# A decoder step's attention, rewritten: prompt heads in pairs on the array's halves, sample queries stationary, compression as filler

## What is computed

```python
z = x @ w_in
# mixer A, 8 heads x 64: stick-breaking attention
z = einsum('bthd,bshd->bhts', q, k) * SCALE
log_keep = where(mask, log_sigmoid(-z), 0)
cum = cumsum(log_keep); after = cum[..., -1:] - cum
o_a = where(mask, exp(log_sigmoid(z) + after), 0) @ v
# mixer B, 8 query heads in 2 groups: three softmax branches (compressed, selected, window)
blk = t[:, idx] + cmp_pe               # 15 blocks of 32 rows, stride 16, per sequence and group
ck, cv = gelu(blk @ cmp_w1) @ cmp_w2   # compressed keys and values
o_b = g0 * softmax(q ck) cv + g1 * softmax(q sk) sv + g2 * softmax(q wk) wv
# then, unchanged by the edit
m = concat(rms(o_a), rms(o_b)) @ w_out; h = LN(alpha*x + m)
y = LN(alpha*h + PEER(h))              # 16384 experts, top 16 of 8 heads
```

## Time and profile before

| | |
|---|---|
| median of 3 runs | 1209.02 us (1208.8 to 1218.2) |
| profiled execution | 1215.3 us, span 1213.2 us |
| PE busy | 1170.7 us (96%) |
| PE weight loads | 1029.2 us (85%) |
| DVE, ACT, POOL busy | 870.0, 580.8, 253.5 us |
| chain that ended last | PE 79%, DVE 8%, DMA 5%, issue 5% |

### The profile page before, as it was taken

The page is one execution under the profiler, slowest core; times in us unless marked ns, Lnnn a source line. Parts: engine busy times, 40 slices in busy tenths (PEclk is TensorE's granted clock), DMA queues, the critical chain, the costliest instruction groups (busy, mean ns, idle before and its releaser), DMA issues.

```text
span 1213.2 us, 23944 instructions
## 1 busy us (share of the span) xinstructions
PE 1170.7 (96%) x7404; PEld 1029.2 (85%) x7404; DVE 870.0 (72%) x1835; ACT 580.8 (48%) x1091; POOL 253.5 (21%) x264
## 2 busy tenths in 40 slices
PE   7999999999989999999999999998999999999996
PEld 7984787767879999999999999997878778788875
DVE  4320124324578898888775699997999989887777
ACT  5432753324444544444446455554555555555543
POOL 0425000003000010004540000001545555442330
PEclk9999875559989999999999999999999999999998
DMA  7758311001433578779998554445899989887772
GB/s 249 286 165 292 112 66 70 1 1 52 139 104 123 175 235 293 234 226 335 407 407 269 179 151 136 145 145 177 276 322 305 296 294 307 299 268 244 240 238 82
DMA packets 96361, 253.11 MB, mean 209 GB/s; under 512 B 11168, under 2 KB 43984, under 8 KB 95648
## 3 DMA queue, kind: packets, MB, share of 16 engines
q1 hardware_dynamic: 81840, 196.86, 49.2%
q0 software_dynamic: 14480, 55.75, 13.1%
HBM read 232.51 MB, written 22.12 MB: 210 GB/s over the span
## 4 chain that ended last, share of the span: by engine, by line
PE 79%; DVE 8%; DMA 5%; issue 5%; ACT 2%; POOL 1%; DVEq 0%; SPq 0%; ACTq 0%; POOLq 0%
PE ps L535 13%; PE ps L537 12%; PE ps L536 12%; PE ps L944 6%; PE ps L946 6%; PE ps L945 6%; PE ps L925 5%; DMA activations<-u_out 4%; DVE w_lo L1311 4%; PE ps L631 3%; PE ps L778 2%; DVE sacc L1745 1%; PE ps L658 1%; PE ps L764 1%; PE ps L871 1%
## 5 line engine op out<-in xcount | busy, mean ns | idle before, releaser
L1311 DVE TENSOR_TENSOR w_lo<-ring,w_hi 128x512 fp32r<-128x512 f32 (+1 forms) x458 | 430.2, 949 | 115.0 <-ACT w_hi L998 99.0
L998 ACT CAST w_hi<-ring 128x512 fp32r<-128x512 f32 (+1 forms) x460 | 344.2, 752 | 95.0 <-PE ps L946 49.7
L535 PE MATMUL ps<-h_hi,w_hi 128*128 128x256 f32 (+1 forms) x1152 | 339.9, 295 | 6.5 <-DVE h_lo L1572 4.9
L537 PE MATMUL ps<-h_hi,w_lo 128*128 128x256 f32 (+1 forms) x1152 | 326.7, 284 | 0.0
L536 PE MATMUL ps<-h_lo,w_hi 128*128 128x256 f32 (+1 forms) x1152 | 324.3, 282 | 0.0
L535 PEld LDWEIGHTS ps<-h_hi,w_hi 128*128 128x128 f32 x1152 | 218.2, 189 | 11.7 <-DVE h_lo L1572 5.3
L536 PEld LDWEIGHTS ps<-h_lo,w_hi 128*128 128x128 f32 x1152 | 218.2, 189 | 0.0
L537 PEld LDWEIGHTS ps<-h_hi,w_lo 128*128 128x128 f32 x1152 | 217.4, 189 | 0.0
L944 PE MATMUL ps<-w_hi,y_hi 128*128 128x512 f32 x512 | 201.1, 393 | 10.0 <-DVE y_lo L1733 9.2
L945 PE MATMUL ps<-w_hi,y_lo 128*128 128x512 f32 x512 | 200.0, 391 | 0.0
L946 PE MATMUL ps<-w_lo,y_hi 128*128 128x512 f32 x512 | 199.8, 390 | 0.0
(11 more groups left out here) (347 smaller groups left out, 1447.4 us busy)
## 6 DMA issues: line engine op xcount, KB each, us to landing
ring<-in_uT_dram SPq DMA_DIRECT2D x128, 512.0 KB
ring<-in_v_dram SPq DMA_DIRECT2D x128, 512.0 KB
activations<-u_out SPq DMA_DIRECT2D x128, 128.0 KB
a_in<-activations SPq DMA_DIRECT2D x128, 128.0 KB, 4.2
ring<-in_w_in_dram SPq DMA_DIRECT2D x22, 512.0 KB
kvs<-in_cache_sb_dram POOLq DMA_DIRECT2D x16, 512.0 KB, 7.0
ring<-in_w_q_dram SPq DMA_DIRECT2D x16, 512.0 KB
ring<-in_w_out_dram SPq DMA_DIRECT2D x8, 512.0 KB
```

The source lines that it names most:

```text
L535: mm(out, hi, hi_, start=start, stop=False)
L537: return mm(out, lo, hi_, start=False, stop=stop)
L998: nc.scalar.copy(w_hi[slot][:, x], ring[:, ring_slot, x]).then_inc(part_hi, 2 if half is None else 1)
L1311: V.tensor_tensor(w_lo[slot][:, x], ring[:, ring_slot, x], w_hi[slot][:, x].bitcast(F32), ALU.subtract).then_inc(part_lo[ring_slot], 2 if ...
```

## The change

Attention's list is rewritten on all engines; the projection, the output projection and the experts keep theirs.

- Prompt heads go in pairs p (two heads of 64 on the rows or columns 0 to 63 and 64 to 127 of the array): the two matmuls of a pair stand next to each other and write two banks (scores) or the two column halves of one bank (values). The `block` mask is added by DVE before the softplus, so the two mask products of `sb_sums` and the two `keep` multiplications go.
- ACT loads one table set that holds Exp and Ln, ahead of the loops, and does Abs, Exp, Ln on a pair (768 columns); the scaling of queries goes into ACT's copy out of the projection.
- The compression matmuls read 15 neighbouring elements per sequence. For that POOL copies the gathered pages into that layout (two `tensor_copy` of 2048 elements per partition), and only then issues the rest. The 32 matmuls are cut into 8 parts and stand between the steps of the stick-breaking pairs.
- Sample scores and values: queries or weights (32 columns per sequence) are stationary, cached keys and values move (256 or 512 columns); four sequences use the four column strips of the array. Scores then lie with rows on the partitions, so 6 transposes turn them (`zrow`), and for the values a mask (`picked`) and 8 small products (`tokrow`) pick each head's part.
- The loop over the softmax heads goes in 4 pairs; the transposes of the compressed weights stand in `np_turn` (8 transposes instead of 6).
- The closing sample value products are reordered so that four sequences stand next to each other.
- POOL's DMAs: `nsk` right after the copies, keys (16) and values (8 and 8) as separate half pages, the window cache earlier, the 2 MB output copy last. Issues of pages grow from 48 to 64.

```diff
             for n in range(PAGES):
-                b, p = n // 2, n % 2
-                pool.dma_start(cmpT[:, 2 + 2 * b:4 + 2 * b, :, 64 * p:64 * p + 64].rearrange("p g k n -> p (g k) n"),
-                               src(cache_cmp, n).rearrange("a p g k n -> (a p) (g k) n")).then_inc(cmp_in, 16)
-            pool.wait_ge(w_mm, 2 * N_IN)
-            for n in range(PAGES):
-                pool.dma_start(kvs[:, n, :], src(cache_sb, n).rearrange("a p c -> (a p) c")).then_inc(kv_in[n // 4], 16)
+                pool.dma_start(pages_in[:, n // 2, n % 2, :, :],
+                               src(cache_cmp, n).rearrange("a p w c -> (a p) w c")).then_inc(cmp_in, 16)
+            pool.wait_ge(cmp_in, 16 * (PAGES + 1))
+            for p in range(2):
+                nc.gpsimd.tensor_copy(
+                    cmpT[:, 2:2 + 2 * NB, :, :, 8 * p:8 * p + 8].rearrange("q (b g) k m a -> q b (g k) m a", g=2),
+                    pages_in[:, :, p, :, :]).then_inc(cmp_laid, 1)
+            pool.wait_ge(cmp_laid, 2)
             for n in range(PAGES):
                 pool.dma_start(nsk[:, n, :], src(cache_nsa, n).rearrange("a p c -> (a p) c")).then_inc(nsk_in, 16)
...
+            def sb_scores(p):
+                if p >= 2:
+                    pe.wait_ge(sb_arg, p - 1)
+                b = 1 + 2 * (p % 2)
+                for x, keys_, q0 in ((slice(0, 256), slice(0, 128), 0), (slice(256, 384), slice(128, 256), 128)):
+                    for g in range(2):
+                        half = slice(g * HD, (g + 1) * HD)
+                        ins = mm(ps[:, b + g, x], zT[half, KA + p, keys_], zT[half, p, q0:256], start=True, stop=True)
+                ins.then_inc(sb_qk, 1)
...
+            def compress(part):
+                j = part // 4
+                for m in range(4 * (part % 4), 4 * (part % 4) + 4):
+                    blocks = cmpT[:, :, j, m % 8, m // 8:m // 8 + NC_]
+                    ins = mm(ps[:, 5 + j, 0:(2 * NSEQ + 1) * NC_], w1s[:, j, m, :], blocks, start=m == 0, stop=m == 15)
...
+            compress(0)
+            compress(1)
+            sb_sums(0)
+            compress(2)
+            sb_sums(1)
+            compress(3)
+            sb_scores(2)
...
+            for w in range(2):
+                pe.wait_ge(k_in[w], 16 * 8)
+                for hp in range(4):
+                    for b in range(4 * w, 4 * w + 4):
+                        mm(ps[b % 4 * 32:b % 4 * 32 + 32, w, 0:PAST], qs[:, hp, 32 * b:32 * b + 32],
+                           ks[:, 2 * b:2 * b + 2, hp * 128:(hp + 1) * 128], start=hp == 0, stop=hp == 3)
...
+            for r in range(4):
+                np_turn(2 * r)
+                if r < 3:
+                    np_scores(r + 1)
+                np_turn(2 * r + 1)
+                if r < 2:
+                    if r == 0:
+                        pe.wait_ge(ss_w, 1)
+                    ss_values(r)
...
+                np_values(r)
```

More of the change, by code:

```diff
@@ L309, in trunk @@
         x_in = [sem(f"x_in{q}") for q in range(4)]
[L310 removed]
+        k_in = [sem(f"k_in{q}") for q in range(2)]
+        v_in = [sem(f"v_in{q}") for q in range(2)]
         x_h, x_l, o_h, o_l = map(sem, ("x_h", "x_l", "o_h", "o_l"))
@@ new lines, in _, with ns_scores @@
+            ins.then_inc(ss_qk, 1)
+            sb_values(2)
+            sb_values(3)
+            def ns_scores(br, keys_of):
+                for b in range(NB):
+                    rows = slice(b % 4 * 32, b % 4 * 32 + 32)
+                    mm(ps[rows, (3, 0)[br] + b // 4, 0:PAST], qbd_b[:, b, :], keys_of(b), start=True, stop=True)
+                for w in range(2):
+                    mm(ps[:, (3, 0)[br] + w, PAST:PAST + 32], qbd_b[:, 4 * w:4 * w + 4, :],
+                       zT[:, (SK, WK)[br], TP:T], start=True, stop=True)
@@ L752, in np_turn, with np_values @@
+                for tt in range(2):
+                    ins = nc.tensor.transpose(ps[0:NC_, 4 + tt, 384:512], sc_[:, 8 * g + 2 * r + tt, :], ident)
                 ins.then_inc(np_t, 1)
-            def np_values(n):
-                r, g = HEADS[n]
-                half = slice(g * HD, (g + 1) * HD)
-                h = g * 4 + r
-                b = 6
-                pe.wait_ge(np_pt, n + 1)
-                if g == 0 and r >= 1:
+            def np_values(r):
+                pe.wait_ge(np_pt, 2 * r + 2)
+                if r >= 1:
@@ L1066, in _ @@
+            for rows, c in parts:
+                ins = A(lss[rows, c], lss[rows, c], ACT.Exp, scale=-1.0)
+            link(ins)
+            for rows, c in parts:
+                ins = A(lss[rows, c], lss[rows, c], ACT.Ln, bias=1.0)
+            ins.then_inc(ss_ln, 1)
             act.wait_ge(ckv_mm, 2)
             for m in range(3):
-                w = min(4, NSEQ - 4 * m)
-                ins = nc.scalar.copy(cv[:, 4 * m:4 * m + w, :],
-                                     ps[0:NC_, (0, 5, 6)[m], 0:w * 128].rearrange("p (s n) -> p s n", n=128))
+                w, row = ((4, 0), (4, 0), (1, 32))[m]
+                ins = nc.scalar.copy(cv[:, 4 * m:4 * m + w, :], ps[row:row + NC_, (7, 6, 6)[m], 0:w * 128].rearrange(
+                    "p (s n) -> p s n", n=128))
@@ L1071, in _ @@
             ins.then_inc(ckv_sb, 1)
-            sb_exp(0)
-            for h in range(1, 8):
-                if h + 1 < 8:
-                    sb_soft(h + 1)
-                sb_exp(h)
-            act.wait_ge(ss_qk, 1)
-            act.wait_ge(sb_arg, 8)
-            parts = ((slice(0, 128), slice(0, 512), 0), (slice(0, 32), slice(512, 768), 7))
-            for rows, c, b in parts:
-                w = c.stop - c.start
-                nc.scalar.copy(zb[rows, c], ps[rows, b, 0:w])
-                link(A(lb[rows, c], ps[rows, b, 0:w], ACT.Abs))
@@ L1086, in _ @@
-            for rows, c, b in parts:
-                link(A(lb[rows, c], lb[rows, c], ACT.Exp, scale=-1.0))
-            for rows, c, b in parts:
-                ins = A(lb[rows, c], lb[rows, c], ACT.Ln, bias=1.0)
-            ins.then_inc(ss_ln, 1)
-            act.wait_ge(nc_s, 1)
-            A(sc_[:, :, :], sc_[:, :, :], ACT.Exp).then_inc(nc_e, 1)
-            act.wait_ge(ss_arg, 1)
-            act.wait_ge(sb_pv, 8)
-            for rows, c, b in parts:
-                ins = A(wb[rows, c], ab[rows, c], ACT.Exp)
@@ L1113, in np_exp @@
                 ins.then_inc(np_e, 1)
+            act.wait_ge(nc_s, 1)
+            A(sc_[:, :, :], sc_[:, :, :], ACT.Exp).then_inc(nc_e, 1)
             np_exp(0)
@@ L1118, in _ @@
                     np_exp(n + 1)
-                if n == 1:
+                if n == 0:
+                    act.wait_ge(ss_arg, 1)
+                    for rows, c in parts:
+                        ins = A(zss[rows, c], zss[rows, c], ACT.Exp)
+                    ins.then_inc(ss_w, 1)
+                if n == 2:
                     act.wait_ge(ns_s, 1)
```

636 lines of the change are left out of this document (329 added, 307 removed).

## The result

| | before | after |
|---|---|---|
| median | 1213.61 us (4 runs, 1208.8 to 1218.2) | 1140.88 us (4 runs, 1138.44 to 1145.2) |
| profiled execution | 1215.3, span 1213.2 | 1141.7, span 1140.0 |
| granted clock over the span | 0.949 | 0.972 |

The ratio is 0.9407, with a 95% interval of 0.9353 to 0.9462. The prediction had 1133.4 from the median and 1139.7 from the profiled execution, which came to 1141.7. Between the two profiles the first matmul with `w_out` moved from 296.6 to 216.4 us, 80.2 earlier, but the end moved by 73.2 only. So two things want an explanation: where the 80.2 came from, and where 7.0 went in a stretch whose instructions the edit doesn't touch.

A forecast was written before the change was run, and what follows sets the result against it. PE was taken to bound attention; A 39.9, B 30 and C 53 us saved 67.8, the closing part 7.8: 75.6 off 1209.02 gives 1133.4 us. Forecast 1125 to 1145, range 1113 to 1165.

The forecast's parts named there:

- A: Stage from 85.2 us to the end of the sample scores, with compression and stick-breaking: predicted 39.9 us, ending at 125.1.
- C: The softmax loop, 72 us before: predicted 53 us, with 11.1 of gaps and 27.1 of work at clock 0.65.
- B: Stage from the sample scores to the loop's first transposes: kept at 30 us, with ends 25 and 38.
- closing part: Sample value products after the softmax loop: 12 us before, 4.2 predicted with groups of four strips, 7.8 saved.
- the rest after it: From the first tile of `w_out` to the end: keeps its length, so attention's saving comes off one for one.
- Compression: In A: 32 matmuls at 0.52 us each with neighbouring columns, 16.6 instead of 33.1 us.
- The rival without overlap: Pairs and strips don't overlap: 1158 us if only pairs don't, 1191 if accumulating strips don't either; chance 0.11.
- POOL's queue: Copies before compression 4.7 us each, ending at 79 to 80; waits of 0 to 5 us for keys, 0 to 8 for `kv_out`.
- The slower rival: POOL's two copies hold up everything: the gain is eaten at 43 us each, 1227 us at 52 each; chance 0.03.
- Table loads: Rival on ACT: loads between Exp and Ln stay, 10.3 us on ACT, 4 counted, 1137 us; chance 0.04.
- The rival at the full clock: Full clock in B and C: B 25 and C 38, 20 us more saved, 1113 us; chance 0.15.
- The rule on PSUM: Skill's warning for the softmax loop: PSUM evacuation may bind; DVE's 7.1 us a pair stays under PE's 9.0 to 14.3.

The follow-up runs named there:

- run 1: The changed kernel with compression's columns 8 elements apart again, as in the old layout: 1158.59 us, ratio 0.9529.
- run 7: The kernel before with only the closing sample value products reordered, four sequences of one step next to each other: 1203.17 us, ratio 0.9927.
- Run 4: The changed kernel with the two heads of a pair one after the other in all four products instead of alternating: 1156.33 us, ratio 0.9495.
- run 6: The changed kernel with POOL's two copies of the compression input made six times, 20 us more on its queue: 1155.65 us, ratio 0.9509.
- run 5: The changed kernel without the two requests for the table set that holds both Exp and Ln: 1146.2 us, ratio 0.9432.
- run 12: The changed kernel with 240 words of padding behind the constants and `h_lo` moved up by 240 words too: 1144.35 us, one run.
- Run 11: The changed kernel with 4 needless matmuls of 256 columns before each of the loop's three waits for the second turn: 1134.08 us, ratio 0.9343.
- runs 9: The changed kernel with 240 words of padding, so all buffers except the constants and `h_lo` lie at their old addresses: 1137.19 us, ratio 0.9373.
- run 2: The changed kernel with sample values and picks moved in front of the softmax loop's second turn: 1132.2 us, ratio 0.9296.
- run 3: As run 2, with the value products of the pair before put off into the gap too: 1142.31 us, ratio 0.9389.

## Why the prediction was right, and what it had wrong

The forecast and its range held. The limits named for each stage were the right ones in A and C; the sizes were off in both directions, and the closeness of the total is partly luck. Up to the first `w_out` matmul the terms were 4.6 us too long together: 8.6 in A and B, less 2.5 in C, less 1.5 by which attention started later than in the profile before (86.7 for 85.2). Behind it 7.0 us came that the prediction had at nothing. The two nearly cancel.

The 80.2 us came from A and B (118.6 us before, 61.3 after: 57.2, of which run 1 gives 17 to the compression columns), C (16.5), and the closing part (7.9), less the later start. The share of C depends on the execution: with the loop of run 7 before it, it would be 8.9.

| term | predicted | measured |
|---|---|---|
| A | 39.9 | 36.5 |
| B | 30 | 24.8 |
| C | 53 | 55.5 |
| closing products | 4.2 | 4.0 |
| first `w_out` matmul | near 221 | 216.4 |
| the rest after it | unchanged, 916.6 | 923.6 |

- **Compression** at 0.52 us a matmul: 0.49, and run 1 shows that the distance of the columns is the cause.
- **Pairs and strips overlap**: scores 0.9 and 0.86, values 0.8 and 0.80, a strip group 0.47 and 0.46. The rival without overlap had the pairs 6.6 us longer in A and 18 in C. Run 4, which spoils the overlap, has nothing in A and 16.1 in the loop; that its 1156.33 lies near the rival's 1158 is chance.
- **A** was 3.4 too long: the 2 us put in for waits didn't come, compression took 0.9 less and the four pairs of sums 1.75 each for 1.9.
- **POOL's queue**: a copy took 2.0 us where I had taken 4.7 from a row with two inputs, so that they ended at 72.5 and not at 80. The slower rival (43 us a copy) was far off; its mechanism is real. For the keys run 6 confirms the point from which it decides, an end of the copies near 80. For `kv_out` it puts it near 74: the prediction had this wait in B, at 0 to 8 us, but not in the rival's 80, and the queue was one microsecond from binding.
- **B**: the 30 us were taken over from the old stage, which ran at a clock of 0.50 throughout (173.81 to 203.79). The new one runs at 1.00 up to 134 us, and ends at 24.8, at the prediction's own bound of 25 for the full clock. The compressed keys, values and scores took 4.3 us (129.69 to 134) instead of about 7. The wait of 0 to 8 us for `kv_out` didn't come, by half a microsecond. It is DVE and its hand-overs that last in the end of B (waits of 2.89 and 4.40 us), not PE.
- **Table loads**: none between Exp and Ln. Priced 4 if they stay, measured 5.3 by the medians and 3 by the ratios (run 5).
- **C**: the sum was 11.1 us of gaps and 27.1 / 0.65 of work, 53 in all; measured are 12.7 of waits and 42.8 of work, which ran at a mean clock of 0.65 (the 0.72 of the row has the waits in it). The gap of 3.7 came as 3.43, three times, but two waits for ACT in the last pair, 1.23 and 1.14, were not in the sum. The 0.65 was chosen between two arguments that no row weighs, so that it fits is luck: the same instructions took 58.3 us in run 12. The rival at the full clock, with all its gaps and C at 38, had an assumption that the runs speak against. Run 11 shows that the gaps themselves hold the clock down. A gap costs its own 3.4 us and slows what follows it. With the gaps partly filled the clock is 0.96 and the loop 44.8, with 6 us of added work in it and 8.5 us of waits left.
- **The rule on PSUM.** That DVE would set the loop, by the Trainium skill (TensorEngine Tiling (Array Packing), section PSUM Bottleneck), isn't borne out as throughput: DVE is busy for 24.92 us even of run 11's 44.8. Its latency is: what PE waits for at the three gaps of 3.4 us is DVE's chain of bias and scaling.
- **"Projection, output projection and experts are untouched by the edit", so "what attention saves comes off the end one for one"**: this step failed. 4.5 of the 7.0 us are the slower matmuls of `h_lo` and `w_hi`, due to a buffer that moved (runs 9 and 12). The other 2.5 stay open. With the old placement the new kernels still took 919.9 and 920.4 us there, where both kernels with the old attention took 916.6; with the new placement executions range from 918.7 to 924.5, in part by short waits for `w_lo`.

What stays open is how the chip sets the clock, so that one loop takes 64.4 or 72.0 us; and the placement's cause, where other distances weren't tried. No run isolates the sample products with queries or weights stationary, nor the mask that left `sb_sums`; for these the durations of their rows are the evidence.

## What to carry to other kernels

Read idle gaps on PE twice: once for their own length and once for the granted clock of what follows them. A stretch's mean clock has its gaps in it, so take the gaps out before dividing work by it. Before calling a DMA queue free, ask for the slack of each thing on it (run 6). A hand-over gap is worth filling with work that is due anyway (run 2, 5.5 us of the loop), and then not with so much that the next gap opens (run 3). Interleave the two halves of the array instruction by instruction, and keep a moving operand's columns together in memory. When an edit changes the size of a table, compare the mean durations of the stages that it doesn't touch, form by form.

## What the runs showed of the hardware

- Three idle gaps of 3.4 us on PE in a loop of 55.5 went with a granted clock of 0.72, 0.65 while PE was busy; with 4 matmuls in each gap it was 0.96, and the loop got 10.7 us shorter though it held more work. The Trainium skill (TensorE: Matmul & The Clock Gate, section Why this matters for your kernels) advises to avoid idle gaps between bursts of matmuls; the trace agrees, with 44.8 us for 55.5.
- Where a buffer lies changed one kind of matmul by 4 ns in 279 (1.5%), over 1024 of them.
- Halves of the array overlap for two instructions a side in a row (0.80 us for a pair's values) but hardly for four (2.3 for 1.5 us) and not for five (4.0 for 2.0 us).
- A POOL copy of 2048 fp32 in runs of 8 elements took 2.0 us, less than the 2.37 of a two-input operation on 1024.
